# Making fourteen weight sums with a copying and an adding transfer instead of a GpSimd addition

## The reference, cut to what matters

```python
def channel_mlp(h, w_in, w_out):
    return jnp.square(jax.nn.relu(h @ w_in)) @ w_out
...
f_lat = channel_mlp(modulate(x_lat, g_pre_mlp[i], m_lat[3], m_lat[4]), w_mlp_in[i], w_mlp_out[i])
x_lat = x_lat + m_lat[5] * rms_norm(f_lat, g_post_mlp[i])
```

## Time and profile before

| What | Value |
|---|---|
| Median of three runs | 2273.26 us |
| Span of the profiled execution, first to last instruction | 2269.7 us |
| TensorE busy | 2229.6 us, 98% of the span |
| VectorE busy | 1432.9 us, 63% |
| ScalarE busy | 488.6 us, 22% |
| GpSimd busy | 286.7 us, 13% |
| The 14 additions of L3472, all together | 35.4 us |
| The 14 subtractions of L3474, all together | 34.7 us |

### The profile page before, as it was taken

One profiled execution on the slowest core, in us unless ns is written; L12 is line 12 of the kernel. 1 busy time (PEld: TensorE's weight loads), 2 busy tenths in 40 slices (PEclk: granted clock), 3 DMA queues, 4 the chain that ended last, 5 costly groups with the idle time before them and its releaser, 6 DMA issues.

```text
span 2269.7 us, 30050 instructions
## 1 busy us (share of the span) xinstructions
PE 2229.6 (98%) x12022; PEld 1819.5 (80%) x12022; DVE 1432.9 (63%) x2592; ACT 488.6 (22%) x1067; POOL 286.7 (13%) x181
## 2 busy tenths in 40 slices
PE   7999999999999999999999999999999999999998
PEld 5888598799868885988998655588888887768987
DVE  5774355744656566756656777775575468766655
ACT  1212230100012222201010265321200023343300
POOL 0000011422000001213210000000000001001442
PEclk9999999999999999999999999999999999999999
DMA  9883338654576655465655411433433324445542
GB/s 392 296 301 132 112 131 315 228 181 143 203 276 193 246 186 204 155 233 186 195 196 175 170 38 38 158 112 130 146 134 129 118 96 167 131 167 186 177 167 84
DMA packets 179770, 398.77 MB, mean 176 GB/s; under 512 B 21168, under 2 KB 25648, under 8 KB 176560
## 3 DMA queue, kind: packets, MB, share of 16 engines
q1 hardware_dynamic: 136736, 285.03, 35.7%
q0 software_dynamic: 24080, 93.69, 11.9%
q10 hardware_dynamic: 18816, 18.12, 2.5%
HBM read 395.71 MB, written 1.11 MB: 175 GB/s over the span
## 4 chain that ended last, share of the span: by engine, by line
PE 92%; DVE 4%; DMA 1%; ACT 1%; issue 0%; POOL 0%; SPq 0%; DVEq 0%; ACTq 0%
PE bank L600 90%; PE bank L598 3%; DVE arena L2240 2%; DVE arena L2246 2%; DMA arena<-in_w_ada 1%; ACT arena L1540 1%; DVE junk L2246 0%; DVE arena L2243 0%; ACT L1540 0%; ACT arena L1543 0%; DVE arena L2836 0%; POOL arena L3472 0%; POOL arena L3474 0%; DVE arena L3238 0%; SPq L3408 0%
## 5 line engine op out<-in xcount | busy, mean ns | idle before, releaser
L600 PE MATMUL bank<-arena 128*128 128x256 f32 (+4 forms) x11438 | 2169.5, 357 | 17.2 <-DVE arena L2240 7.1
L600 PEld LDWEIGHTS bank<-arena 128*128 128x128 f32 (+2 forms) x11438 | 1753.4, 189 | 412.7 <-issue 224.8
L2240 DVE TENSOR_TENSOR arena<-arena 128x1024 f32<-128x1024 f32 (+6 forms) x567 | 476.6, 856 | 204.0 <-PE bank L600 170.2
L1540 ACT ACTIVATE arena<-arena 128x512 f32<-128x512 f32 (+5 forms) x443 | 222.6, 525 | 803.7 <-DVE arena L2240 471.1
L2246 DVE SCALAR_TENSOR_TENSOR arena<-arena 128x1028 f32<-128x1028 f32 (+6 forms) x367 | 317.0, 880 | 96.0 <-DMA arena<-in_w_ada 72.9
L2240 DVE TENSOR_TENSOR arena<-arena,bank 128x256 f32<-128x256 f32 (+2 forms) x382 | 171.8, 475 | 182.1 <-PE bank L600 171.1
L3504 POOL DMA_DIRECT2D arena<-in_w_ada x88 | 63.0, 716 | 1400.2 <-DVEq L2255 1354.0
L1540 ACT ACTIVATE arena<-bank 128x256 f32<-128x256 f32 (+1 forms) x129 | 53.0, 429 | 565.4 <-PE bank L600 564.8
L1543 ACT ACTIVATE arena<-bank 128x512 f32<-128x512 f32 (+1 forms) x163 | 88.4, 599 | 308.7 <-PE bank L600 270.4
L2240 DVE TENSOR_TENSOR arena<-bank,arena 128x512 f32<-128x512 f32 (+2 forms) x95 | 60.4, 646 | 127.7 <-PE bank L600 111.2
L2246 DVE SCALAR_TENSOR_TENSOR arena<-bank,arena 128x254 f32<-128x254 f32 (+2 forms) x184 | 78.1, 469 | 69.1 <-PE bank L598 35.4
(11 more groups left out here) (39 smaller groups left out, 272.3 us busy)
## 6 DMA issues: line engine op xcount, KB each, us to landing
arena<-in_w_ada POOLq DMA_DIRECT2D x88, 1028.0 KB, 5.9
arena<-in_w_in SPq DMA_DIRECT2D x84, 1024.0 KB, 7.4
arena<-in_w SPq DMA_DIRECT2D x56, 1024.0 KB, 7.2
arena<-in_w_mlp_in SPq DMA_DIRECT2D x32, 1024.0 KB, 7.3
arena<-in_w_mlp_out SPq DMA_DIRECT2D x32, 1024.0 KB, 7.0
arena<-in_w_gla SPq DMA_DIRECT2D x12, 1024.0 KB, 6.9
arena<-in_w_ada SPq DMA_DIRECT2D x16, 514.0 KB, 19.5
arena<-in_w_a SPq DMA_DIRECT2D x8, 1024.0 KB, 7.1
```

Of the source, the lines that this page charges most:

```text
L600: ins = nc.tensor.matmul(out, lhsT, rhs, start=start, stop=stop)
L1540: return nc.scalar.activation(out, x, f, **kw)
L2240: return V.tensor_tensor(out, x, y, op)
```

## The change: two transfers in the place of one addition

For the 14 panels the addition at L3472 is replaced by two transfers that GpSimd issues. The first copies a21 into the place of the sum. GpSimd waits until it has landed. The second reads a22 and adds it into that place. GpSimd waits until that one has landed too and then makes the subtraction as before. Both transfers count 16 on a new semaphore, `mlp_first_sum`; TensorE's product 5 waits for it (32 for each panel). `mlp_sums_made` now counts one for each panel and is waited for by product 7 and by VectorE's sum 6.

There are two places for the sum, used in turn (`first_sums`): a new one just behind the hidden activations, and the old `wsum`. So the copy for panel number `at` waits for the readers of panel `at` - 2 rather than of panel `at` - 1, and the first one waits for the end of GLA's output product, whose input had lain where the new place is.

```diff
+        first_sums = [area(G0 + MT * T, KH, 2 * P), wsum]
...
-                if i in (5, 7) and (Progress.phase, name) in POOL_PANELS:
-                    pe.wait_ge(mlp_sums_made, 2 * POOL_PANELS[Progress.phase, name] + (1 if i == 5 else 2))
+                if i == 5 and (Progress.phase, name) in POOL_PANELS:
+                    pe.wait_ge(mlp_first_sum, 32 * POOL_PANELS[Progress.phase, name] + 32)
+                elif i == 7 and (Progress.phase, name) in POOL_PANELS:
+                    pe.wait_ge(mlp_sums_made, POOL_PANELS[Progress.phase, name] + 1)
...
                 if made is not None and i == 6:
-                    dve.wait_ge(mlp_sums_made, 2 * made + 2)
+                    dve.wait_ge(mlp_sums_made, made + 1)
+                    wsum = first_sums[made % 2]
...
-                    fifth = "mlp out 0 5" if before == "mlp out 0 3" else f"{before} 5"
-                    pool.wait_ge(pe_of["gla"], PE.of("gla", f"{fifth} full"))
-                    pool.wait_ge(dve_of["gla"], DV.of("gla", f"{before} w6"))
-                    nc.gpsimd.tensor_tensor(wsum, a21, a22, ALU.add).then_inc(mlp_sums_made, 1)
-                    pool.wait_ge(mlp_sums_made, 2 * at + 1)
+                    if at:
+                        before = names[at - 1]
+                        fifth = "mlp out 0 5" if before == "mlp out 0 3" else f"{before} 5"
+                        pool.wait_ge(pe_of["gla"], PE.of("gla", f"{fifth} full"))
+                        pool.wait_ge(dve_of["gla"], DV.of("gla", f"{before} w6"))
+                    else:
+                        pool.wait_ge(pe_of["gla"], PE.of("gla", "mix 1 1 full"))
+                    pool.dma_start(first_sums[at % 2], a21).then_inc(mlp_first_sum, 16)
+                    pool.wait_ge(mlp_first_sum, 32 * at + 16)
+                    pool.dma_start(first_sums[at % 2], a22, accum_op=ALU.add).then_inc(mlp_first_sum, 16)
+                    pool.wait_ge(mlp_first_sum, 32 * at + 32)
                     nc.gpsimd.tensor_tensor(a21, a11, a21, ALU.subtract).then_inc(mlp_sums_made, 1)
```

More of the change, by code:

```diff
@@ L288, in program @@
         mlp_sums_made = sem("mlp_sums_made")
+        mlp_first_sum = sem("mlp_first_sum")
         masks_in, first_free = sem("masks_in"), sem("first_free")
@@ L1093, in operands, with sum_at @@
                 return {1: (q[0], b11), 2: (q[1], b21), 4: (q[3], T4), 5: (wsum, T1), 7: (q[2], b12), 6: (q[0], T2), 3: (q[1], b22)}
+            def sum_at(name):
+                at = POOL_PANELS.get((Progress.phase, name))
+                return wsum if at is None else first_sums[at % 2]
             def wait_for(i, name, t_name):
@@ L1110, in up @@
                 def up(p, i):
-                    ops = operands(quarters(first_of[l, "w_mlp_in"] + 2 * p), x, *tcomb)
+                    ops = operands(quarters(first_of[l, "w_mlp_in"] + 2 * p), x, *tcomb, sum_at(f"{tag} in {p}"))
                     key = f"{tag} in {p} {i}"
@@ L1143, in fast_mlp @@
                         apart = nh == T and (p, kg) == (1, 3)
-                        ops = operands(q, x, late_tokens, *tcomb[1:], late_sum) if apart else operands(q, x, *tcomb)
+                        ops = operands(q, x, late_tokens, *tcomb[1:], late_sum) if apart else operands(q, x, *tcomb, sum_at(f"{tag} out {p} {kg}"))
                         def down(i, p=p, kg=kg, ops=ops):
@@ L3463, in mlp_sums @@
                 names = [f"mlp in {p}" for p in range(1, MLP // PW)] + [f"mlp out {p} {kg}" for p in range(2) for kg in range(4)]
-                for at, (before, name) in enumerate(zip(names, names[1:])):
+                for at in range(len(names) - 1):
                     n = first_of[1, "w_mlp_in"] + 4 + 2 * at
```

## The result

| | us |
|---|---|
| Before, median of four runs | 2272.50 (2271.72 to 2273.48) |
| After, median of four runs | 2315.23 (2313.23 to 2320.54) |
| Ratio after / before | 1.0187, 95% interval 1.0175 to 1.0200 |
| Forecast | 2287.7, range 2280 to 2335 |

The change makes the kernel 42.7 us slower. The sign was forecast and the time lies in the range, but the loss is three times the 14.4 us of the forecast. The mechanism that decided was the one called B, and it was larger than the 32.6 us put down for it. In the table of the experiments one run of e5 is left out, a run of 2927.26 us with a mean granted clock of 0.75 where the others of e5 have 0.99.

What follows compares the result with a forecast made beforehand. TensorE was taken to bound the kernel. A first-panel delay of 12.7 us plus 1.7 us of clock made 14.4 us, added to the 2269.7 us span and 3.6 us for the runs' median: 2287.7 us, range 2280 to 2335.

Steps and rivals of the forecast that it cites:

- B: Rival: loads push the transfer chain over the 12.08 us period in later panels; 32.6 us more at 13.5 us, chance 0.34.
- What bounds the kernel, and what there is to gain: Last MLP: TensorE bounds; GpSimd's work costs only where TensorE waits, so at most 1.29 us can be gained.
- The first panel: Start of the last MLP: copy and add not hidden, TensorE idle 13 us, product 7 of `mlp in 2` 12.7 us later.
- The clock's loss: Behind the first panel's idle time TensorE runs four microseconds at a granted clock of 0.57, losing 1.7 us.
- The price of the chain on quiet engines: Each panel's copy, add, subtraction and waits on GpSimd take 11.8 us, with bounds of 7.8 and 21.2 us.
- As long as it is shorter, later panels are hidden: Panels after the first: an 11.8 us chain under the 12.08 us period costs nothing; each microsecond above costs thirteen.
- The period: Late in the last MLP, GpSimd's additions start 12.08 us apart, one panel of seven TensorE products.
- There is room, but where they overlap with a load both slow down: Last MLP's engines, free about half the time, can take the new transfers' added share of 0.33.
- A: The forecast itself: one stall at the start, then a hidden chain; 8 to 18 us more, chance 0.46.
- Rival C: The adding transfer is near its upper bound, the chain takes 18 us; 91 us more, chance 0.08.
- Rival D: Not slower: the first two transfers land in 2.6 us each, under 7 us together; 2276.1 us, chance 0.06.

Runs made afterwards that it cites:

- e5: Changed kernel with the first panel's copy, add and subtraction moved ahead of the last transfer of modulation weights on GpSimd's list; 2316.72 us.
- e11: Kernel before with GpSimd additions in two places, no transfers, the first panel's two instructions ahead of the last modulation weights; 2273.47 us.
- e2: Changed kernel with the two transfers for the first panel only and GpSimd's addition for the other 13; 2291.51 us.
- e3: Changed kernel with the last MLP's weight loads cut from 1 MB to 256 KB from its fourth panel on; 2291.62 us.
- e6: Changed kernel with each panel's copy issued as soon as the add of the panel before is issued; 2289.68 us.
- e8: Changed kernel with the last gate row written to HBM in runs of 32 bytes instead of 1024 pieces of 4 bytes; 2308.57 us.
- e9: Changed kernel with GpSimd's addition for the first two panels and the two transfers for the other 12; 2301.46 us.
- e1: Changed kernel with its two places and looser waits, but GpSimd's addition in place of the two transfers; 2278.45 us.

## Why the prediction was wrong, point by point

- **What bounds the kernel, and what there is to gain**: right. e11 takes GpSimd off TensorE's path without any transfer, and the time is the same.
- **The first panel**: right in its sum. TensorE's idle piece was forecast as 13 us and is 13.16. Its parts were off in opposite ways: the copy landed 8.1 us after issue, not 9.8, and the add took 7.1 us, not 5.2, with loads still running beside it (DMA share 1.07 at 2102 to 2106, where the forecast had quiet engines). The clock's loss was forecast as 1.7 us and is 2.5. Idle time and clock together make 14.7 us against the 14.4 forecast; that the sum fits so well is in part luck. e2's 15.8 us hold 1.9 us of waiting for VectorE besides.
- **The price of the chain on quiet engines**: right. The forecast had 3.9 + 5.2 + 2.35 + 0.3 = 11.8 us. Where few loads are left the subtractions stand 11.4 to 12.1 us apart; with quarter loads copy and add land in 3.4 and 5.7 us in the median.
- **"As long as it is shorter, later panels are hidden"**: this is the step that failed. It set a quiet price of 11.8 us against the period, so the sum has nothing for the 13 later panels. Both prices in it were built on the fastest GpSimd transfer (5.2 us) though the median stood beside it. The two transfers ran among two loads of 1 MB a panel, and their mean chain was 14.53 us. Behind the start about 28 us were lost (42.7 - 14.7). e3 takes the crowding away, e6 the length of the chain, and each comes back to the start's loss and 1 to 2 us.
- **The period**: 12.08 us holds for `mlp out` alone; in `mlp in` a panel takes 12.5. The true margin was thus a little larger than forecast, and it did not help: the thirteen chains took 28.9 us more than thirteen periods.
- **"There is room, but where they overlap with a load both slow down"**: the first half is shown by e6, and the second half is what the sum left out. I compared bytes with the engines' idle share, which says nothing on a chain that waits for each landing.
- **Rival B**: the right mechanism with a chance of 0.34, its chain of 13.5 us too short by a microsecond. That the time lies in the stated range is owed to B's part of it; A's own range ended at 18 us. B's picture of about a microsecond of idle time in every panel was wrong. The delays come in lumps, and one of them (8.65 us) comes largely from a write that B did not name, as e8 shows. The next one, 6.44 us, belongs to the add that took 12.0 us; it is there in e5, e8 and e9 as well, with 6.1 to 6.4 us, and gone with the loads cut in e3.
- **Rival C**: the add is slower than the copy, 5.4 us at the least against a forecast of 5.2, but not near its upper bound of 11.8 as a rule: the median is 6.3, and one add in fourteen took 11.9.
- **Rival D**: it failed as argued, by the busy engines at the start: the two transfers together took 15.1 us there, not under 7.

## What to carry to other kernels

A chain of transfers that are waited for one by one is to be priced with landings among the loads of its own stretch, not with the fastest landing in the trace, when it has only a few per cent to spare against the period. Free engine time is no cover for such a chain; issuing the next transfer before waiting for the last one is (e6 against the change: 26 us). Transfers that replace a short instruction where its result is already waited for cost their whole latency there, and a slower clock on top (13.16 us idle and 2.5 us of clock at the start here).

## What the runs showed of the hardware that was not expected

- The adding transfer costs more than a copy of the same size: 5.4 us against 3.3 at the least, and GpSimd is busy for 1.28 us with its issue against 0.80 [the rows of L3486 and L3488 above]. In the trace's packet records the copy goes as 128 packets of 4 KB of 187 ns in the median, the add as 512 packets of 1 KB of 101 ns at the least and 112 in the median. With 16 packets of 4 bytes for each transfer that is 672 for a panel, and the page's count fits (9408 packets more on GpSimd's queue, 14 x 672).
- 1024 pieces of 4 bytes written to HBM just ahead hold up a copy from SBUF to SBUF by some 6 us (10.7 us against 4.8 in e8, where they are 128 runs of 32 bytes). The last of the small packets starts at 2153.85. From then to 2158.2, 32 of the copy's 128 packets take 0.6 to 3.1 us each; of those of the other thirteen copies one takes over 0.4 us, and in e8's copy none. Why they do is not shown. The engines count as busy then while little moves (the second of these stretches, in the profile after):

```profile
2151.00:2154.00 3.00, 2.76 (x25) 2.79 (x26) 2.77 (x3) 0.00 (x0) 0.84 (x2) 1.00 1.11 370
2154.00:2157.00 3.00, 3.00 (x29) 3.00 (x28) 1.86 (x6) 1.35 (x4) 0.00 (x0) 1.00 1.10 97
```

- Earlier GpSimd additions are not free for TensorE: in e1 they ran beside VectorE's sums, two of which then took 6.64 us instead of 2.56, and TensorE waited 3.6 us for VectorE.
